# Half-tile squares ahead of entry splits in the inner norms, and modulation rows spread evenly over up and down

## The chip, the cores and the metric

One core of one Trainium2 chip runs the whole program. The metric is the device time of one execution in microseconds (us), the median of several runs. Engines: PE (TensorE) multiplies, ACT (ScalarE), DVE (VectorE) and POOL (GpSimd) work elementwise, SP issues the DMAs.

## The reference

A sequence of 512 tokens of width 1024 passes a first block (two layers of mixed attention) and a second block (two layers). The change touches only the second block. Cut to what matters:

```python
def second_block(x, c, w_ada, b_ada, norm_g, w_in, ..., w_out, w_up, conv_w, conv_b, w_down):
    for l in range(DEPTH):
        mod = jax.nn.silu(c) @ w_ada[l] + b_ada[l]
        sh1, sc1, g1, sh2, sc2, g2 = jnp.split(mod[:, None, :], 6, axis=-1)
        h = rms_norm_2(x, norm_g[l, 0]) * (1.0 + sc1) + sh1
        ...
        mix = jnp.concatenate([o_a, o_b, o_c], axis=-1) @ w_out[l]
        x = x + g1 * mix
        h = rms_norm_2(x, norm_g[l, 1]) * (1.0 + sc2) + sh2
        x = x + g2 * conv_ffn(h, w_up[l], conv_w[l], conv_b[l], w_down[l])
    return x
```

`rms_norm_2` divides each token by the root of its mean square over the 1024 channels. `conv_ffn` multiplies by `w_up` (1024 x 5632), convolves three neighbouring tokens, multiplies silu of one half by the other half (2816 channels, 22 tiles of 128), and multiplies by `w_down`.

## The kernel before, in words

**Tiling.** Channels lie on the 128 partitions, tokens along the free axis: x is XT, eight tiles of 128 channels by 512 tokens. Every product is made three times, with high and low parts: weights and values are split into a high part (rounded to fp32r) and the rest, and PE adds high x high, high x low and low x high (`channels`, line 695; `half_products`, line 887, for 256 tokens at a time).

**Weights.** PE's program builds a list `units`. Each unit is one DMA of 128x1024 numbers into one of three buffers RAW (unit n takes RAW[n % 3]; SP issues unit n once unit n-3 is done with it, in the order of the list, line 1760). For a weight, ACT copies the high part into WH, or into a spare tile X, Y or Z (line 1818), and POOL subtracts to get the low part (line 2447), which frees RAW; the ring of WH/WL has two places, given back when PE has used them. On ACT these splits stand at hand-placed points: `ahead(key, by)` issues all splits, in the order of the list, up to the weight of `key` and `by` further; a split that has been issued is not issued again.

**Modulation rows.** The sum silu(c) @ w_ada is made on DVE from rows of w_ada that pass through the same RAW ring as units of their own (not split): line 2742 for the first row of a chunk, line 2744 for the seven others. After eight rows a chunk of 1024 sums is transposed by PE (`modulation_columns`, line 738, eight transposes) and reduced on DVE (`modulation_biases`). In layer 0 of the second block 56 rows (`FEED_ROWS`) go beside up and down: `feed_rows` gives the rows behind up unit n = 2j + s (j over 22 tiles, s over the two halves of the product), `feed_rows_down` those behind unit i of down tile m (a down tile has three weights, i = 0, 1, 2).

**The norm that ends by halves** (`end_by_halves`, one function on each of PE, ACT and DVE). It is used three times: norm ("2",0,"n",1) after `wout` of layer 0, ("2",1,"n",0) after `down` of layer 0, and ("2",1,"n",1) after `wout` of layer 1. The last two output tiles, 6 and 7, are made in halves of 256 tokens:

- PE: (6, first half), (7, first half), then (6, second half) with the sums of squares of the first half in its middle (`half_sums`, lines 895 and 899), then the spread of the root (`half_spread`, line 908), (7, second half), and then three entry units together (line 948): up (0,0), (0,1), (1,0) in tiles X, or bff 0, bfb 0, bff 1 in tiles Y.
- DVE: updates x with each half (line 3101), adds the squares into ACC (line 3062), inverts the root, and writes the normalised value GV (line 3081) and the low part HL (line 3075) for each of eight tiles and both halves.
- ACT: squares the halves (line 2191), takes the root (line 2200), and writes the high part HH (line 1847). Before it, line 1873 loads the table that has the root (`load_root`).

Before the change ACT issues all splits up to the fourth entry unit, then the table load, and then the first square of a half tile.

Of the kernel before, what the change touches and what calls it, by code (L numbers as in the profile page):

```python
# [24 lines left out]
KD = DM // P  # L25
# [20 lines left out]
KF = DFF // P  # L46
# [123 lines left out]
FEED_ROWS = rows_of(("mod2", 0, MOD2_CHUNKS - 1), *[("mod2", 1, c) for c in range(MOD2_CHUNKS)])  # L170
# [25 lines left out]
def program(nc, D, out, known, stop=None):  # L196
    led = Ledger(known)
    up, at = led.up, led.at
    ctx = ExitStack()
    with ctx:  # L200
# [340 lines left out]
        def feed_rows(l, j, s):  # L541

            n = 2 * j + s
            if l or n < 5:
                return []
            return FEED_ROWS[2 * (n - 5):2 * (n - 5) + 2] if n < 10 else FEED_ROWS[n:n + 1]

        def feed_rows_down(l, m, i):

            n = 2 * KF + 2 * m + i  # L550
            return FEED_ROWS[n:n + 1] if l == 0 and i < 2 else []

        def completed(rows):

# [1252 lines left out]
        def _(act):  # L1807
# [18 lines left out]
            def freed(key):  # L1826
                return up(evacuated[led.slot(key)], key)
# [44 lines left out]
            def load_root():  # L1872
                A(SMALL[:, 7:8], epsb[:, 0:1], ACT.Sqrt)
# [304 lines left out]
                                 lambda s: MOD2[l][:, 24 * i + k:24 * i + k + 1],  # L2178
                                 (key, "rows") if k == KD - 1 else None)

            def end_by_halves(norm, name, following):

                _, l, _, i = norm

                def square_half(m, p):
                    if p:
                        value_is_there(None, name + (m,))
                    else:
                        act.wait_ge(dve_step, at(dve_step, (norm, "x", m)))
                    act.wait_ge(dve_step, at(dve_step, (norm, "add", m - 2)))  # L2190
                    A(SQ2[m % 2][:, half(p)], XT[:, m, half(p)], ACT.Square).then_inc(*up(act_out, (norm, "sq", m, p)))

                def shifted(p, k):
                    high_shifted(("2", l, "h", i, p, k), HH2[:, k, :], SEQ, lambda s: MOD2[l][:, 24 * i + k:24 * i + k + 1],
                                 (norm, "rows") if p and k == KD - 1 else None, [(0, HALF * p, HALF)])

                square_half(KD - 2, 0)
                square_half(KD - 1, 0)
                ps = ready((norm, 0))
                A(RCOL[:, 0:2], ps[:, 0:2], ACT.Sqrt, bias=epsb[:, 0:1], scale=1.0 / DM).then_inc(*freed((norm, 0)))  # L2200
                square_half(KD - 2, 1)
                for k in range(KD):
                    if k == 3:
                        square_half(KD - 1, 1)
                    if k == 5:
                        act.wait_ge(product_ready, at(product_ready, (norm, 1)))
                        A(RCOL[:, 2:4], psum[led.slot((norm, "rows"))][:, 1000:1002], ACT.Sqrt, bias=epsb[:, 0:1],
                          scale=1.0 / DM).then_inc(*up(act_out, (norm, 1, "root")))
                    shifted(0, k)
                for k in range(KD):  # L2210
                    shifted(1, k)
                ahead(following)
# [165 lines left out]
            def second_layer(l):  # L2378
                if l == 0:
                    for k in range(KD):  # L2380
                        if k == KD - 1:
                            keep_wide(("2", l, "n", 0), RSTD2, SEQ)
                        square2(l, 0, k, lambda k: updated_tile(act, 1, k), "tiles")
                    norm2(l, 0)
                recurrence(l)
                ahead(("2", l, "wout", 0))
                pair_attention(l, "a")
                pair_attention(l, "c")
                for j in range(3):
                    high(("2", l, "mix", "c", j), XH2[:, 5 + j, :], SEQ, ("2", l, "cyN", j))  # L2390
                for m in range(KD - 2):
                    ahead(("2", l, "wout", m))
                    square2(l, 1, m, lambda k: value_is_there(None, ("2", l, "out", k)), "DVE")
                ahead(("2", l, "wout", KD - 1), 4)
                load_root()
                end_by_halves(("2", l, "n", 1), ("2", l, "out"), ("2", l, "up", 1, 1))
                for j in range(KF):
                    for s in range(2):
                        key = ("2", l, "up", j, s)
                        ahead(key)  # L2400
                        U = (UA, UB)[s]
                        ps = ready(key)
                        if j:
                            act.wait_ge(split_value, at(split_value, ("2", l, "f", j - 1)))
                        c = s * KF + j
                        A(U[:, :], ps[:, 0:SEQ], ACT.Identity, bias=vec("conv_b", l, c),  # L2406
                          scale=vec("conv2", (l, 1), c)).then_inc(*up(act_out, ("2", l, "u", j, s)))
                    ahead(key, 2)
                    value_is_there(None, ("2", l, "up", j, 0))
                    A(UA[:, :], UA[:, :], ACT.Silu).then_inc(*up(act_out, ("2", l, "silu", j)))  # L2410
                    high(("2", l, "f", j), FH[:, j, :], SEQ)
                last = l == DEPTH - 1
                for m in range(KD if last else KD - 2):
                    for i in range(3):
                        ahead(("2", l, "down", m, i))
                    if not last:
                        square2(l + 1, 0, m, lambda k: value_is_there(None, ("2", l, "down", k)), "DVE")
                if not last:
                    ahead(("2", l, "down", KD - 1, 2), 4)
                    load_root()  # L2420
                    end_by_halves(("2", l + 1, "n", 0), ("2", l, "down"), ("2", l + 1) + FIRST_UNITS[3])

            if stop is None or stop[0] == "second":
                for l in range(DEPTH):
# [149 lines left out]
        def _(dve):  # L2574
# [519 lines left out]
            def end_by_halves(norm, name, gate):  # L3094

                l = name[1]

                def updated(m, p):
                    key, x = name + (m,), XT[:, m, half(p)]
                    dve.wait_ge(product_ready, at(product_ready, half_key(name, m, p)))  # L3100
                    ins = V.scalar_tensor_tensor(x, psum[led.slot(key)][:, 512 * p:512 * p + HALF],
                                                 MOD2[l][:, gate + m:gate + m + 1], x, ALU.mult, ALU.add)
                    if p:
                        ins.then_inc(*freed(key))
                        own(key)
                    else:
                        step(ins, (norm, "x", m))

                def second_update():
                    updated(KD - 1, 1)  # L3110
                    add_half(norm, KD - 2, 1)

                def second_root():
                    dve.wait_ge(act_out, at(act_out, (norm, 1, "root")))
                    V.reciprocal(RCOL[:, 2:4], RCOL[:, 2:4]).then_inc(*up(to_pe, (norm, 1, "rows")))

                updated(KD - 2, 0)
                add_half(norm, KD - 3)
                updated(KD - 1, 0)
                add_half(norm, KD - 2, 0)  # L3120
                own((norm, 0))
                V.reciprocal(RCOL[:, 0:2], RCOL[:, 0:2]).then_inc(*up(to_pe, (norm, 0, "rows")))
                updated(KD - 2, 1)
                apply_half(norm, 0, {2: second_update, 5: second_root})
                apply_half(norm, 1, {})
# [198 lines left out]
            def second_layer(l):  # L3324
# [25 lines left out]
                for j in range(KF):  # L3350
# [16 lines left out]
                    gv = value(("2", l, "f", j))  # L3367
                    V.tensor_tensor(gv[:, 0:SEQ], UA[:, :], UB[:, :], ALU.mult).then_inc(*valued(("2", l, "f", j)))  # L3368
                    dve.wait_ge(split_value, led.count[split_value.name])
                for i in range(2):  # L3370
                    modulation_rows(feed_rows_down(l, 0, i))
                last = l == DEPTH - 1
                norm = ("2", l + 1, "n", 0)
# [2 lines left out]
                for m in range(KD if last else KD - 2):  # L3376
                    key = ("2", l, "down", m)
                    dve.wait_ge(product_ready, at(product_ready, ("2", l, "down", m, 2)))
                    ps = psum[led.slot(key)]
                    x = XT[:, m, 0:SEQ]  # L3380
                    V.scalar_tensor_tensor(x, ps[:, 0:SEQ], MOD2[l][:, 40 + m:41 + m], x, ALU.mult, ALU.add).then_inc(  # L3381
                        *freed(key))
                    own(key)
                    if m >= 2 and not last:
                        add_half(norm, m - 1)
                    for i in range(2):
                        modulation_biases(feed_rows_down(l, m, i))
                        if m + 1 < KD:
                            modulation_rows(feed_rows_down(l, m + 1, i))
# [45 lines left out]
```

## Time and profile before

| | us |
|---|---|
| median of 3 runs | 3182.79 |
| lowest and highest | 3179.22, 3186.59 |
| the profiled execution | 3177.08 |
| its span | 3175.3 |
| PE busy in it | 3039.2 (96%) |
| DVE, ACT, POOL busy | 1536.3, 1186.6, 1063.1 |

The span is from the first to the last instruction; the execution's time is 1.8 us more. A matmul's record overlaps the next one's, so a busy PE says only that it had work. In the timeline a row has its start, its duration, engine and line, what it writes and reads, how many instructions are merged in it (x3), and in brackets the idle time of the engine before it with what ended that. PEclk, the granted TensorE clock, is 1.00 at full speed and 0.50 at half.

### The profile page before, as it was taken

How to read it: one execution, taken by the hardware profiler on the slowest of the kernel's cores; microseconds unless marked ns; L12 is line 12 of the kernel's file. 1: busy time of each engine (PE TensorE's matmuls, PEld its weight loads, DVE VectorE, ACT ScalarE, POOL GpSimd, SP SyncE). 2: the span in 40 equal slices, each digit the busy share in tenths (PEclk: the TensorE clock that was granted, in tenths of full speed). 3: DMA queues.
4: the chain of work that ended last, by engine and by line, in shares of the span. 5: the costliest groups of instructions: out<-in, count | busy, mean ns of one | idle time of the engine just before them, and what ended most of it. 6: DMA issues, size and time to landing. Idle time of an engine off the chain costs nothing.

```text
span 3175.3 us, 45245 instructions
## 1 busy us (share of the span) xinstructions
PE 3039.2 (96%) x18354; PEld 2472.1 (78%) x18354; DVE 1536.3 (48%) x1947; ACT 1186.6 (37%) x1937; POOL 1063.1 (33%) x509
## 2 busy tenths in 40 slices
PE   8999999999999999999999999899999999999999
PEld 6867688888888777788876776688888777788887
DVE  4364446462233586523314765377742875454520
ACT  3255421212224355432234445433432435444422
POOL 1302033323343301244452221335545221245553
PEclk9999999999999999999999999999999999999999
DMA  6201025342222233344332212246655112023332
GB/s 216 44 6 41 1 74 139 89 130 61 66 60 60 56 110 89 80 126 115 97 93 75 60 41 63 61 126 188 189 163 151 49 47 69 28 80 95 98 96 91
DMA packets 442379, 279.77 MB, mean 88 GB/s; under 512 B 113610, under 2 KB 419516, under 8 KB 441788
## 3 DMA queue, kind: packets, MB, share of 16 engines
q1 hardware_dynamic: 442172, 276.87, 31.1%
q8 instruction: 147, 2.41, 0.3%
q14 instruction: 60, 0.49, 0.0%
HBM read 274.73 MB, written 2.10 MB: 87 GB/s over the span
## 4 chain that ended last, share of the span: by engine, by line
PE 67%; DVE 4%; POOL 3%; ACT 3%; issue 2%; DMA 1%; DVEq 0%; ACTq 0%; POOLq 0%; SPq 0%
PE ps L695 45%; PE ps L1422 4%; POOL WL L2447 2%; PE ps L948 2%; PE ps L1498 2%; PE ps L1520 2%; PE ps L1491 1%; PE ps L1237 1%; PE ps L1563 1%; ACT WH L1818 1%; PE ps L1247 1%; PE ps L1264 1%; PE ps L1446 1%; PE ps L1594 1%; PE ps L1457 1%
## 5 line engine op out<-in xcount | busy, mean ns | idle before, releaser
L2447 POOL TENSOR_TENSOR WL<-RAW,WH 128x1024 fp32r<-128x1024 f32 (+2 forms) x344 | 827.3, 2405 | 1711.9 <-ACT WH L1818 1700.1
L695 PE MATMUL ps<-HH,WH 128*128 128x512 f32 x2136 | 709.5, 370 | 18.8 <-POOL WL L2447 17.3
L695 PE MATMUL ps<-HH,WL 128*128 128x512 f32 x2136 | 700.9, 366 | 0.0
L695 PE MATMUL ps<-HL,WH 128*128 128x512 f32 x2136 | 700.2, 365 | 0.0
L1818 ACT ACTIVATE WH<-RAW 128x1024 fp32r<-128x1024 f32 (+2 forms) x344 | 356.0, 1035 | 420.0 <-PE ps L695 269.4
L695 PEld LDWEIGHTS ps<-HH,WH 128*128 128x128 f32 x2136 | 367.4, 188 | 99.6 <-POOL WL L2447 25.8
L695 PEld LDWEIGHTS ps<-HH,WL 128*128 128x128 f32 x2136 | 366.4, 188 | 67.4
L695 PEld LDWEIGHTS ps<-HL,WH 128*128 128x128 f32 x2136 | 366.6, 188 | 65.7
L2744 DVE SCALAR_TENSOR_TENSOR XT<-RAW,CS,XT 128x1024 f32<-128x1024 f32 x77 | 129.2, 1677 | 22.5 <-DMA RAW<-in_w_ada 20.9
L695 PE MATMUL ps<-FH,WH 128*128 128x512 f32 x308 | 120.6, 392 | 2.0 <-POOL WL L2447 1.9
L695 PE MATMUL ps<-FH,WL 128*128 128x512 f32 x308 | 120.0, 390 | 0.0
L695 PE MATMUL ps<-FL,WH 128*128 128x512 f32 x308 | 120.0, 389 | 0.0
L2744 DVE SCALAR_TENSOR_TENSOR MSUM<-RAW,CS,MSUM 128x1024 f32<-128x1024 f32 x63 | 110.4, 1787 | 10.4 <-DMA RAW<-in_w_mod 8.7
L1422 PE MATMUL ps<-HH,WH 128*128 128x512 f32 x208 | 91.9, 442 | 3.8 <-POOL WL L2447 3.2
L3381 DVE SCALAR_TENSOR_TENSOR XT<-ps,MOD,XT 128x512 f32<-128x512 f32 x14 | 10.5, 750 | 167.9 <-PE ps L695 167.9
L1237 PE MATMUL ps<-KS,QS 128*128 128x512 f32 (+1 forms) x252 | 86.7, 480 | 3.5 <-ACT GV L1923 2.7
L2455 POOL TENSOR_TENSOR FL<-GV,FH 128x512 fp32r<-128x512 f32 x44 | 57.5, 1307 | 95.8 <-ACT FH L1840 95.8
L2835 DVE TENSOR_REDUCE NMAX<-ps 128x1 f32<-128x768 f32 (+1 forms) x80 | 65.9, 847 | 40.2 <-PE ps L1237 38.9
L1422 PE MATMUL ps<-HH,WL 128*128 128x512 f32 x208 | 82.9, 398 | 0.0
L1422 PE MATMUL ps<-HL,WH 128*128 128x512 f32 x208 | 82.8, 398 | 0.0
L2406 ACT ACTIVATE UB<-ps,VEC 128x512 f32<-128x512 f32 x44 | 34.3, 780 | 125.1 <-PE ps L695 125.1
L1840 ACT ACTIVATE FH<-GV 128x512 fp32r<-128x512 f32 x44 | 27.8, 632 | 141.0 <-DVE GV L3368 141.0
(493 smaller groups left out, 5550.4 us busy)
## 6 DMA issues: line engine op xcount, KB each, us to landing
RAW<-in_w_in SPq DMA_DIRECT2D x122, 512.0 KB, 3.9
RAW<-in_w_ada SPq DMA_DIRECT2D x96, 512.0 KB, 4.0
RAW<-in_w_up SPq DMA_DIRECT2D x88, 512.0 KB, 3.9
RAW<-in_w_in SPq DMA_DIRECT2D x72, 256.0 KB, 3.8
RAW<-in_w_mod SPq DMA_DIRECT2D x32, 512.0 KB, 3.7
RAW<-in_w_down SPq DMA_DIRECT2D x32, 512.0 KB, 3.7
WMOD<-in_w_mod SPq DMA_DIRECT2D x8, 1024.0 KB, 14.1
RAW<-in_w_branch SPq DMA_DIRECT2D x16, 512.0 KB, 3.4
```

The lines of the kernel that those rows point to most:

```text
L695: ins = nc.tensor.matmul(ps[0:width, t0:t0 + tn], a, b[:, k0 + k, tokens0 + t0:tokens0 + t0 + tn], start=first and k == 0 and i == 0, stop ...
L948: ins = nc.tensor.matmul(groups[n][:, half(p)], a, b[:, k, half(p)], start=k == 0 and t == 0, stop=k == KD - 1 and t == 2)
L1237: ins = nc.tensor.matmul(half[:, c:c + m], QS[:, 2 * j + h, qs], KS[2 * j + h][:, start:start + m], start=True, stop=True)
L1422: ins = nc.tensor.matmul(ps[:, 0:SEQ], lhs, rhs[:, k, 0:SEQ], start=k == 0 and i == 0, stop=k == KD - 1 and i == 2)
L1498: ins = nc.tensor.transpose(ps[:, b * P:(b + 1) * P], P2[n % 2][h][:, b * P:(b + 1) * P], ident)
L1520: ins = nc.tensor.matmul(o[hs, qb * P:(qb + 1) * P], VN2[a][:, b, hs], PT2[n % 2][h][:, b * P:(b + 1) * P], start=b == 0, stop=b == NXB - 1)
L1818: A(weight_tiles(units[n][3])[0][:, 0:used], RAW[n % NRAW][:, 0:used], ACT.Copy).then_inc(*up(w_high))
L2406: A(U[:, :], ps[:, 0:SEQ], ACT.Identity, bias=vec("conv_b", l, c), scale=vec("conv2", (l, 1), c)).then_inc(*up(act_out, ("2", l, "u", j, s)))
L2447: nc.gpsimd.tensor_tensor(wl[:, 0:used], RAW[n % NRAW][:, 0:used], wh[:, 0:used].bitcast(F32), ALU.subtract).then_inc(*up(w_low))
L2455: nc.gpsimd.tensor_tensor(L, GV[n % 2][:, 0:T], H.bitcast(F32), ALU.subtract).then_inc(*up(split_low, key))
L2744: V.scalar_tensor_tensor(total, row, c, total, ALU.mult, ALU.add).then_inc(*done)
L2835: V.tensor_reduce(NMAX[:, 2 * n + h:2 * n + h + 1], ps[:, 0:keys], AX.X, ALU.max, negate=True).then_inc(*up(to_act, ("B", l, n, h)))
```

## The change

Three edits, in ACT's order of work and in the placement of modulation rows. (1) After `wout`, the splits of tile 7's weight and of the first entry unit stand before the square of tile 5, instead of behind it. The table load stands directly behind that square; then come the split of the second entry unit, the square of tile 6, the split of the third, the square of tile 7, the root, and only then the split of the fourth, ahead of the second half's square. (2) After `down`, the table load stands before the three entry splits, both squares behind them, and the fourth split behind the root. (3) One modulation row goes behind every up unit from n = 5 on (before: two for n = 5 to 9, then one), so that unit n has row n - 5 instead of row n; the 17 rows left go behind all three units of a down tile (before: 12 rows, behind two of three). PE's, POOL's and SP's programs differ only by the place of the rows.

```diff
         def feed_rows(l, j, s):
 
             n = 2 * j + s
-            if l or n < 5:
-                return []
-            return FEED_ROWS[2 * (n - 5):2 * (n - 5) + 2] if n < 10 else FEED_ROWS[n:n + 1]
+            return FEED_ROWS[n - 5:n - 4] if l == 0 and n >= 5 else []
 
         def feed_rows_down(l, m, i):
 
-            n = 2 * KF + 2 * m + i
-            return FEED_ROWS[n:n + 1] if l == 0 and i < 2 else []
+            n = 2 * KF - 5 + 3 * m + i
+            return FEED_ROWS[n:n + 1] if l == 0 else []
...
-            def end_by_halves(norm, name, following):
+            def end_by_halves(norm, name, splits, following):
...
+                load_root()
+                ahead(splits[0], 0)
                 square_half(KD - 2, 0)
+                ahead(splits[1], 0)
                 square_half(KD - 1, 0)
                 ps = ready((norm, 0))
                 A(RCOL[:, 0:2], ps[:, 0:2], ACT.Sqrt, bias=epsb[:, 0:1], scale=1.0 / DM).then_inc(*freed((norm, 0)))
+                ahead(splits[2], 0)
                 square_half(KD - 2, 1)
...
                 for m in range(KD - 2):
-                    ahead(("2", l, "wout", m))
+                    ahead(("2", l, "wout", m), 1 if m < KD - 3 else 3)
                     square2(l, 1, m, lambda k: value_is_there(None, ("2", l, "out", k)), "DVE")
-                ahead(("2", l, "wout", KD - 1), 4)
-                load_root()
-                end_by_halves(("2", l, "n", 1), ("2", l, "out"), ("2", l, "up", 1, 1))
+                after = [("2", l, "up", j, s) for j in range(2) for s in range(2)]
+                end_by_halves(("2", l, "n", 1), ("2", l, "out"), after[1:4], after[3])
...
                 if not last:
-                    ahead(("2", l, "down", KD - 1, 2), 4)
-                    load_root()
-                    end_by_halves(("2", l + 1, "n", 0), ("2", l, "down"), ("2", l + 1) + FIRST_UNITS[3])
+                    ahead(("2", l, "down", KD - 1, 2), 0)
+                    after = [("2", l + 1) + unit for unit in FIRST_UNITS[0:4]]
+                    end_by_halves(("2", l + 1, "n", 0), ("2", l, "down"), (after[2], after[2], after[3]), after[3])
...
-                for i in range(2):
+                for i in range(3):
                     modulation_rows(feed_rows_down(l, 0, i))
...
-                    for i in range(2):
+                    for i in range(3):
                         modulation_biases(feed_rows_down(l, m, i))
                         if m + 1 < KD:
                             modulation_rows(feed_rows_down(l, m + 1, i))
```

## Rows read from the trace of the kernel before

**Rows 1.** The head of the page
```profile
span 3175.3 us, 45245 instructions
```

**Rows 2.** Timeline of PE, its gaps at the three norms (start, duration, ..., [idle before <- releaser])
```profile
2053.04 0.39 PE L887 MATMUL ps<-MIXH,WH 128*128 128x256 f32 x1 [2.10 <-POOL WL L2447]
2063.95 0.98 PE L895 MATMUL ps<-CONST,ACC 128*128 128x1 f32 x4 [6.33 <-DVE ACC L3062]
...
2456.67 0.98 PE L895 MATMUL ps<-CONST,ACC 128*128 128x1 f32 x4 [4.43 <-DVE ACC L3062]
...
2784.90 0.39 PE L887 MATMUL ps<-MIXH,WH 128*128 128x256 f32 x1 [2.09 <-POOL WL L2447]
2795.39 0.99 PE L895 MATMUL ps<-CONST,ACC 128*128 128x1 f32 x4 [4.44 <-DVE ACC L3062]
```

**Rows 3.** Timeline of ACT ahead of the first norm's root
```profile
2044.07 1.04 ACT L1818 ACTIVATE Z_H<-RAW 128x1024 fp32r<-128x1024 f32 x1
...
2049.50 1.05 ACT L1818 ACTIVATE WH<-RAW 128x1024 fp32r<-128x1024 f32 x1
...
2056.89 1.06 ACT L1818 ACTIVATE X_H<-RAW 128x1024 fp32r<-128x1024 f32 x1 [4.38 <-DMA RAW<-in_w_up]
2060.05 1.06 ACT L1818 ACTIVATE WH<-RAW 128x1024 fp32r<-128x1024 f32 x1 [2.10 <-DMA RAW<-in_w_up]
2061.12 1.28 ACT L1873 ACT_TABLE_LOAD   x1
...
2062.53 0.70 ACT L2191 ACTIVATE SQ<-XT 128x256 f32<-128x256 f32 x2
```

**Rows 4.** Timeline of POOL in the first norm, low half of tile 7's weight
```profile
2050.63 2.36 POOL L2447 TENSOR_TENSOR WL<-RAW,WH 128x1024 fp32r<-128x1024 f32 x1 [3.05 <-ACT WH L1818]
```

**Rows 5.** Timeline of DVE in the first norm
```profile
2051.57 1.97 DVE L3062 TENSOR_TENSOR ACC<-ACC,SQ 128x512 f32<-128x512 f32 x1
2056.29 0.48 DVE L3101 SCALAR_TENSOR_TENSOR XT<-ps,MOD,XT 128x256 f32<-128x256 f32 x1 [2.75 <-PE ps L887]
...
2068.59 0.48 DVE L3101 SCALAR_TENSOR_TENSOR XT<-ps,MOD,XT 128x256 f32<-128x256 f32 x1 [2.24 <-PE ps L887]
```

**Rows 6.** Timeline of SP's queue in the first norm: the DMA of up (1,0)
```profile
2053.01 0.37 SPq L1760 DMA_DIRECT2D RAW<-in_w_up  x1
```

**Rows 7.** Timeline of PE, third norm, second sums at full clock
```profile
2806.60 0.50 PE L895 MATMUL ps<-CONST,ACC 128*128 128x1 f32 x4
...
2807.41 0.36 PE L948 MATMUL ps<-HH,X_H 128*128 128x256 f32 x1
```

**Rows 8.** Windows, first norm: PE, PEld, DVE, ACT, POOL busy, PEclk, DMA share, GB/s
```profile
2064.00:2068.00 4.00, 4.00 (x19) 4.00 (x20) 0.17 (x1) 0.26 (x1) 0.00 (x0) 0.50 0.48 131
```

**Rows 9.** Timelines of ACT, POOL and DVE in the second norm
```profile
2445.14 3.11 ACT L1818 ACTIVATE Y_H<-RAW 128x1024 fp32r<-128x1024 f32 x3 [4.70 <-PE ps L1667]
...
2448.64 5.20 POOL L2447 TENSOR_TENSOR Y_L<-RAW,Y_H 128x1024 fp32r<-128x1024 f32 x2
...
2450.91 0.48 DVE L3101 SCALAR_TENSOR_TENSOR XT<-ps,MOD,XT 128x256 f32<-128x256 f32 x1 [1.66 <-PE ps L887]
```

**Rows 10.** Timelines of ACT and PE in up: units 5, 11, 43, one chunk's transposes
```profile
2107.53 0.78 ACT L2406 ACTIVATE UB<-ps,VEC 128x512 f32<-128x512 f32 x1 [1.61 <-PE ps L695]
...
2149.66 0.78 ACT L2406 ACTIVATE UB<-ps,VEC 128x512 f32<-128x512 f32 x1 [2.79 <-PE ps L695]
...
2328.97 0.78 ACT L2406 ACTIVATE UB<-ps,VEC 128x512 f32<-128x512 f32 x1 [2.53 <-PE ps L695]
...
2130.79 1.04 PE L738 MATMUL ps<-CONST,XT 128*128 128x128 f32 x8
```

**Rows 11.** Timelines of PE, DVE and ACT in down
```profile
2341.30 0.50 PE L695 MATMUL ps<-FH,WH 128*128 128x512 f32 x1 [1.13 <-POOL WL L2447]
...
2380.88 3.19 DVE L2744 SCALAR_TENSOR_TENSOR XT<-RAW,CS,XT 128x1024 f32<-128x1024 f32 x1 [0.71 <-DMA RAW<-in_w_ada]
...
2388.89 1.06 ACT L1818 ACTIVATE WH<-RAW 128x1024 fp32r<-128x1024 f32 x1 [4.62 <-PE ps L695]
```

## The prediction

> **What bounds the kernel now.** I read the page first, then the PE timeline for its idle gaps, then ACT, POOL, DVE and SP around each. PE decides the time, so only gaps in PE, and stretches in which it is granted its lower clock, can be won. In the second block five gaps belong to the three norms that end by halves [rows 2]: before the first norm (layer 0, after `wout`) PE waits 2.10 us for the low half of the last weight tile and 6.33 us for the square sums; the third norm (layer 1, after `wout`) repeats it with 2.09 and 4.44; the second (after `down`) has 4.43 alone. The reader is to see who ends these waits: DVE's addition into ACC, which waited for ACT's squares. In the first norm ACT squares at 2062.53 what DVE had updated at 2056.29 + 0.48 = 2056.77 [rows 3, 5]. In between ACT did splits of entry weights (2056.89 and 2060.05, both after waiting for a DMA) and a table load. That is the stall. After it PE runs at half clock: 0.50, the lower of its two levels (1.2 GHz), over 2064 to 2068 [rows 8].
>
> The up stage of layer 0 has a loss of its own. Unit n's output is taken by ACT at 2107.53 (n=5), 2149.66 (n=11) and 2328.97 (n=43) [rows 10]. From 11 to 43 there are 32 units and four finished chunks, each of these with eight transposes of 1.04 us in all [rows 10]: (179.31 - 4.16) / 32 = 5.47 us a unit, and one modulation row a unit is carried without loss. From 5 to 11, with two rows a unit, six units and one chunk take 42.13 where 6 x 5.47 + 1.04 = 33.9 would do: 8.2 us lost.
>
> **Part 1, first norm.** The splits of tile 7 and of up (0,0) now come before the square of tile 5. Between tile 6's split (2044.07 + 1.04) and that square, straight before 2049.50, ACT had nothing to do [rows 3]. Its buffer was given back with tile 4, so I put it at 2045.1 to 2046.1 and up (0,0) behind it to 2047.2; the square still comes on time, about 2049. POOL then works without a pause, at 2.36 us a tile [rows 4]: tile 6's low half from 2045.2 to 2047.6, tile 7's to 2049.95, up (0,0) from there. So tile 7's low half is there 1 us before PE wants it at 2050.94: the 2.10 us go. ACT's table load and root take 1.28 + 0.2 from 2049.5 to 2051.0 [rows 3], in time that was idle or is now free.
> The DMAs move as well, since SP reuses a RAW buffer when POOL is done with it: up (1,0) was issued at 2053.01, as tile 7's split ended, and ACT took it at 2056.89, 3.9 us later [rows 6, 3]. Now it is issued at 2049.95 and is there at 2053.8. Its split (1.06) holds ACT to 2054.9, and the square of tile 7's first half follows to 2055.3.
> PE: 24 + 12 products take from 2053.04 to the stall at 2063.95 - 6.33 = 2057.62, 0.127 us each [rows 2]. Starting at 2050.95 it reaches the sums at 2055.5. DVE updates the tile at 2054.2 to 2054.7 and then must add with both inputs in SBUF. What that costs beside POOL: the 128x512 addition at 2051.57 ended at 2053.54, only after POOL's operation of 2050.63 to 2052.99 [rows 4, 5]. The third split POOL then has at hand (up (0,1), ready at 2052.6) ends at about 2055.5, and the addition at 2055.8. PE begins the sums at 2055.95: 0.4 us of stall are left. Shift 2.10 + 6.33 - 0.4 = 8.0.
> On this pair of engines the Trainium skill ("SBUF — State Buffer", section "Who interferes with whom") says that the later of the two fully blocks until the other's instruction is done. The trace agrees; it speaks against the change, since more POOL splits now lie next to DVE's adds. By it alone the addition could stand behind two splits instead of one, which is the second rival.
> Clock: from the sums to DVE's update of the next half are 2068.59 - 2063.95 = 4.64 us [rows 2, 5]. At full clock the sums take 2807.41 - 2806.60 = 0.81 [rows 7], twelve products 1.53 and the hand-over 0.1: 2.4. A 0.4 us stall should not lower the clock, so 2.2 more. The fourth split (up (1,1)) now stands behind the root, ahead of the second half's square. Its DMA (issued when up (0,0)'s split ends, 2052.6, there by 2056.5) is earlier than the end of the root, 2055.95 + 0.81 + 0.3 = 2057.1; the split lasts to 2058.2, and DVE's update, on which the next square waits, to 2055.95 + 2.4 + 0.48 = 2058.8. So ACT loses nothing, with 0.6 in hand. But POOL's 2.36 us now run while DVE writes the first HL half, again with two SBUF inputs: I count 0.3 between 0 and one whole split, 2.4. Sum: 8.0 + 2.2 - 0.3 = 9.9.
> **Part 1, third norm.** The same with its own rows: 2.09 + 4.44, and the way between its two stalls took 2795.39 - 4.44 - 2784.90 = 6.05 where the first norm took 4.58, so 1.5 was lost to the clock. 8.0 - 0.4 + 2.2 - 0.3 = 9.5.
> **Part 1, second norm.** Only the fourth split leaves the way, and the table load goes ahead of the three Y splits. These are done at 2448.25, DVE's update of tile 7 at 2450.91 + 0.48 = 2451.39 [rows 9]. POOL does the last two Y splits from 2448.64 to 2453.84, so it changes over at about 2451.5. If the addition (issued at 2451.43) gets in between, the sums meet PE at 2452.24 and the whole 4.43 and the clock's 2.2 are won, less 0.3: 6.3. If not, it ends at 2454.15: 2.4 won, and of the 2.2 about a half, since a gap of 2.1 us was once followed by the low clock (third norm) and once not (first): 3.2. The trace can't tell; I take 4.7.
> **Part 2, rows.** One row a unit from n=5 on: the 8.2 us go, as after n=11. Up finishes one chunk fewer (1.04 less), down one more. Row 39's chunk now ends behind unit (0,0) of down, where PE waits for DVE's row. The unit ends at 2328.97 + 5.47 = 2334.4; DVE comes to the row only behind the last product of up. I put the wait at 0.7, between 0 and 2. With the transposes that is 1.7, but PE then stalls less at 2341.30, where it waits 1.13 for a split [rows 11]. The reduction of that chunk on DVE, 1024 columns as a row has, stands ahead of the row whose buffer tile 1's third weight needs: up to 0.9. Together 8.2 + 1.0 - 1.7 + 1.1 - 0.9 = 7.7.
> Every down tile now carries three rows in three units. A row can hold DVE for 3.19 us behind POOL [rows 11]; the next tile's first weight waits for the second row's buffer: from the row's end at 2384.07 plus 3.9 it is there at 2388.0, and ACT takes the next tile's first weight at 2388.89, when PE gives back the slot [rows 11]. So it is just covered, by 0.9; with that cover gone each tenth of a microsecond counts, in five tiles. I count nothing, the range 0 to 4.
>
> **Sum.** 9.9 + 9.5 + 4.7 + 7.7 = 31.8. The profiled execution took 3177.1 (span 3175.3 [rows 1]); it would take 3145.3. The median of the runs lies 5.7 above it, so I set 3182.8 - 31.8 = 3151.
>
> **Rivals.** (1) The forecast: chance 0.60, 3143 to 3159 by the terms' ends (second norm 3.2 or 6.3, down 0 to 4, stalls 0 to 1, runs differing by 4).
> (2) The addition comes behind POOL's next split: 2.36 us more in norms one and three, and with gaps of some 2.7 the clock falls again (2.2 each), with the second norm at 3.2: 9.1 + 1.5 = 10.6 less, 3162. For it: adds and splits are within 0.8 us. Against: in the trace the waiting addition gets in at the first change-over. 0.18.
> (3) The third row per down tile brings back what the second row a unit cost in up: 1.4 us for each of six units there, once or twice in each of five tiles, 7 to 14 less: 3158 to 3165. Against it: two DMAs a unit, not three. 0.12.
> (4) It doesn't do what it says: the square of tile 7 stays behind a weight whose DMA lands 3 us or more after my 2053.8, because transfers that now follow 2.4 us apart share the engines. Then the gaps stay, and only part 2 is won: 3175. Against: landing took 3.9 at a like density. 0.06.
> (5) Slower: the ring of three RAW buffers locks to DVE's rows in down. If the next weight is issued only after the row that follows the tile's own update, its DMA, split and POOL pass (3.9 + 1.06 + 2.36 = 7.3) lie open in each of five tiles, 36.6 in all: 3151 + 37 = 3188. It decides when the third row is eaten later than the end of the next tile, 15 us; I find 11. 0.04.
>
> Range: leaving out (4) and (5) and the far end of (3), 3142 to 3166. A difference of 0.2%, 6.4 us, is about what a measurement can tell: faster 0.93, same 0.04, slower 0.03.
>
> **What would show it.** Right: no PE gap over 1 us ahead of tile 7 in norms one and three; sums there 0.4 us late; clock 1.00 throughout; ACT's squares 0.1 us after DVE's updates or after the split of up (1,0); no PE gap in up between n=5 and n=11; gaps in down below 1.2 us each, as the one in [rows 11]. Wrong: a gap of 2 us and more at the sums behind a POOL pass (2), PE waiting for `down` weights whose DMA follows a row (3, 5), ACT waiting for RAW between the two squares (4).

## The result and the profile after

The changed kernel takes 3152.26 us (median of five runs, 3150.69 to 3155.84); in the same session the kernel before took 3179.22 to 3187.32, and the ratio is 0.9901 (95% interval 0.9889 to 0.9912). One run of the kernel before, of 6019 us, and one of the rows alone below, of 7639 us, were disturbed and are outside the ratios. The forecast was 3151, the range 3142 to 3166.

The profiled execution took 3152.26; its page begins so, where the kernel before had 3175.3 [rows 1]:

```profile
span 3150.5 us, 45245 instructions
PE 3037.7 (96%) x18354; PEld 2466.8 (78%) x18354; DVE 1544.4 (49%) x1947; ACT 1186.1 (38%) x1937; POOL 1065.5 (34%) x509
```

Work and counts are the same; what shrank is waiting, and the time that PE spent at its lower clock. **Where the time went** is read best by taking the same PE instruction in both traces and subtracting its start: the number changes only in a stretch that became shorter or longer. Steps of that difference, in us, worked out from the PE timelines of each kernel against the one of the kernel before:

| stretch | after | squares alone | rows alone | 4th split early | 4th split late | both squares first |
|---|---|---|---|---|---|---|
| first block and all up to the first norm | +6.8 | -3.7 | +7.9 | +0.9 | +2.9 | +4.5 |
| first norm, to the sums | -7.9 | -8.0 | -0.2 | -7.9 | -8.0 | -8.9 |
| first norm, behind the sums | -2.6 | -2.6 | +0.1 | +0.9 | -2.5 | -2.4 |
| entry and up, to n = 5 | -1.0 | +0.2 | -1.1 | -1.1 | -0.5 | +1.1 |
| up, n = 5 to 11 | -7.9 | +2.4 | -7.7 | -7.9 | -7.8 | -7.9 |
| up, n = 11 to the start of down | +1.0 | +0.8 | +1.4 | +0.8 | +0.9 | +0.9 |
| down | +0.1 | 0.0 | +1.5 | +1.9 | -0.4 | -0.5 |
| second norm, to the sums | -4.6 | -4.6 | -0.1 | -4.6 | -4.6 | -4.6 |
| second norm, behind them | -2.5 | -2.5 | +1.1 | +0.5 | -2.6 | -2.5 |
| between second and third norm | +3.3 | -0.5 | +3.2 | +2.1 | +1.6 | +0.5 |
| third norm, to the sums | -7.5 | -7.5 | 0.0 | -7.5 | -7.5 | -8.4 |
| third norm, behind them | -2.0 | -2.0 | +0.7 | +1.0 | -2.1 | +0.5 |
| from there to the end | 0.0 | 0.0 | 0.0 | 0.0 | +0.6 | +1.2 |

In the changed kernel the stretches that the change touches give 10.5 (first norm), 7.8 (up and down), 7.1 and 9.5: 34.9 together. The two rows of untouched work give back 10.1 in this one execution. The first differs from -3.7 to +7.9 over kernels whose code is the same there, so it is the spread of executions and no effect; the medians have less of it. ("Rows alone" is read from its second run, the one with a usable trace.)

PE's gaps at the three norms, as [rows 2] (timeline of PE, the kernel after; ACC is the sum of squares):

```profile
2062.78 0.58 PE L893 MATMUL ps<-CONST,ACC 128*128 128x1 f32 x4 [0.75 <-DVE ACC L3063]
...
2440.57 0.50 PE L893 MATMUL ps<-CONST,ACC 128*128 128x1 f32 x4
...
2772.61 0.58 PE L893 MATMUL ps<-CONST,ACC 128*128 128x1 f32 x4 [0.76 <-DVE ACC L3063]
```

The gaps of 2.10 and 2.09 for tile 7's weight are gone without a row of their own, 6.33 has become 0.75, 4.43 nothing, 4.44 has become 0.76. ACT in the first norm, as [rows 3], and POOL, as [rows 4]:

```profile
2050.84 1.04 ACT L1816 ACTIVATE Z_H<-RAW 128x1024 fp32r<-128x1024 f32 x1
2051.78 1.04 ACT L1816 ACTIVATE WH<-RAW 128x1024 fp32r<-128x1024 f32 x1
2052.73 1.04 ACT L1816 ACTIVATE X_H<-RAW 128x1024 fp32r<-128x1024 f32 x1
2055.74 0.63 ACT L1857 ACTIVATE SQ<-XT 128x512 f32<-128x512 f32 x1 [1.96 <-DVE XT L3345]
2056.39 1.28 ACT L1871 ACT_TABLE_LOAD   x1
...
2058.17 1.06 ACT L1816 ACTIVATE X_H<-RAW 128x1024 fp32r<-128x1024 f32 x1 [0.29 <-DMA RAW<-in_w_up]
2059.13 0.40 ACT L2189 ACTIVATE SQ<-XT 128x256 f32<-128x256 f32 x1
2061.09 1.06 ACT L1816 ACTIVATE X_H<-RAW 128x1024 fp32r<-128x1024 f32 x1 [1.55 <-DMA RAW<-in_w_up]
2062.05 0.40 ACT L2189 ACTIVATE SQ<-XT 128x256 f32<-128x256 f32 x1
...
2056.68 8.19 POOL L2448 TENSOR_TENSOR X_L<-RAW,X_H 128x1024 fp32r<-128x1024 f32 x3
```

Three splits stand back to back ahead of tile 5's square, the table load sits in idle time, and the two half-tile squares follow one split each. Tile 7's square comes at 2062.05, 0.87 after DVE's update of 2060.70 + 0.48; in the kernel before the two squares began 5.8 after it. The window behind the sums, as [rows 8], is at the full clock:

```profile
2064.00:2068.00 4.00, 4.00 (x36) 4.00 (x35) 2.54 (x6) 2.50 (x5) 3.27 (x2) 1.00 0.82 240
```

DVE in the first and the second norm, as [rows 5] and [rows 9], with POOL in the second:

```profile
2060.70 0.48 DVE L3102 SCALAR_TENSOR_TENSOR XT<-ps,MOD,XT 128x256 f32<-128x256 f32 x1 [0.60 <-PE ps L885]
2061.22 1.42 DVE L3063 TENSOR_TENSOR ACC<-ACC,SQ 128x256 f32<-128x256 f32 x1
...
2067.03 0.78 DVE L3076 SCALAR_TENSOR_TENSOR HL<-GV,MOD,HH 128x256 fp32r<-128x256 f32 x1
...
2439.92 0.43 DVE L3063 TENSOR_TENSOR ACC<-ACC,SQ 128x256 f32<-128x256 f32 x1
...
2434.77 7.82 POOL L2448 TENSOR_TENSOR Y_L<-RAW,Y_H 128x1024 fp32r<-128x1024 f32 x3 [2.96 <-ACT Y_H L1816]
```

The same addition takes 1.42 behind a POOL pass and 0.43 where it meets a change-over (three passes from 2434.77 in 7.82: the second change-over is at about 2440.0). In up PE has no gap above 0.05 between n = 5 and n = 11, and unit 5 and unit 11 lie 32.98 apart where [rows 10] had 42.13 (ACT takes their outputs). Of these 9.15 the table has 1.1 in the row above n = 5, since its cut there stands behind the first of the gaps that went:

```profile
2103.88 0.78 ACT L2407 ACTIVATE UB<-ps,VEC 128x512 f32<-128x512 f32 x1 [3.06 <-PE ps L693]
...
2136.86 0.78 ACT L2407 ACTIVATE UB<-ps,VEC 128x512 f32<-128x512 f32 x1 [2.53 <-PE ps L693]
```

In down, as [rows 11], PE waits 0.36 for the row whose chunk it transposes. The product that waited 1.13 in the kernel before starts at 2329.91 without any idle time, so that wait is gone. The next wait for a split, 0.43 in the kernel before, is 0.48:

```profile
2323.51 1.09 PE L736 MATMUL ps<-CONST,XT 128*128 128x128 f32 x8 [0.36 <-DVE XT L2745]
...
2329.91 0.39 PE L693 MATMUL ps<-FH,WH 128*128 128x512 f32 x1
...
2340.09 0.50 PE L693 MATMUL ps<-FH,WH 128*128 128x512 f32 x1 [0.48 <-POOL WL L2448]
```

The last of these in the kernel before:

```profile
2351.55 0.50 PE L695 MATMUL ps<-FH,WH 128*128 128x512 f32 x1 [0.43 <-POOL WL L2447]
```

### The profile page after: what moved, and what is told of

It reads as the page before. It is cut to its first block, busy times and chain, and to the rows that moved or that the text cites. A ratio compares the mean times of both kernels' runs of the same rounds, so it can differ in the third digit from the quotient of the medians.

```text
span 3150.5 us, 45245 instructions
## 1 busy us (share of the span) xinstructions
PE 3037.7 (96%) x18354; PEld 2466.8 (78%) x18354; DVE 1544.4 (49%) x1947; ACT 1186.1 (38%) x1937; POOL 1065.5 (34%) x509
## 3 DMA queue, kind: packets, MB, share of 16 engines
q1 hardware_dynamic: 442172, 276.87, 31.5%
## 4 chain that ended last, share of the span: by engine, by line
PE 68%; DVE 3%; POOL 3%; ACT 3%; issue 2%; DMA 1%; SPq 0%; DVEq 0%; ACTq 0%; POOLq 0%
PE ps L693 46%; PE ps L1420 4%; POOL WL L2448 2%; PE ps L946 2%; PE ps L1496 2%; PE ps L1518 2%; PE ps L1489 1%; PE ps L1235 1%; PE ps L885 1%; PE ps L1561 1%; ACT WH L1816 1%; PE ps L1245 1%; PE ps L1262 1%; PE ps L1303 1%; PE ps L1592 1%
## 5 line engine op out<-in xcount | busy, mean ns | idle before, releaser
L2745 DVE SCALAR_TENSOR_TENSOR XT<-RAW,CS,XT 128x1024 f32<-128x1024 f32 x77 | 140.7, 1827 | 31.2 <-DMA RAW<-in_w_ada 30.2
L3382 DVE SCALAR_TENSOR_TENSOR XT<-ps,MOD,XT 128x512 f32<-128x512 f32 x14 | 10.5, 751 | 141.5 <-PE ps L693 141.5
```

The source lines that it names most:

```text
L2745: V.scalar_tensor_tensor(total, row, c, total, ALU.mult, ALU.add).then_inc(*done)
```

## The experiments

My theory: the gain is ACT's squares no longer waiting behind splits (some 27 us in three norms, 2 us of each being the clock that no longer falls), and 7 to 8 us of modulation rows. Against it stood: one part gives all; the clock part isn't the stall's; the fourth split's place doesn't matter; and a third row in down costs. Ratios are to the kernel before, run beside each.

**Each part alone.** The squares' order with the rows as before, and the rows with the old order (cut; DVE's loops over a down tile's rows go with it, two or three times):

```diff
 squares alone (against after)          rows alone (against before)
-return FEED_ROWS[n - 5:n - 4] ...     +return FEED_ROWS[n - 5:n - 4] if l == 0 and n >= 5 else []
+return FEED_ROWS[2 * (n - 5):...]     -return FEED_ROWS[2 * (n - 5):...]
-n = 2 * KF - 5 + 3 * m + i            +n = 2 * KF - 5 + 3 * m + i
+n = 2 * KF + 2 * m + i                -n = 2 * KF + 2 * m + i
```

> The new order of squares and splits alone; modulation rows placed as in the kernel before. Theory (three separate gains that add): the three norms gain what the changed kernel's trace shows, 10.4, 7.1 and 9.5 us, so 27 us less than before in all; up between units 5 and 11 keeps its loss of 8.2 us, PE gaps of 1 to 2 us with rows' DMAs among them, and down its gap of 1.1 us in tile 0. Rival (the two edits hang together, since rows that come earlier take RAW buffers while the norm's last splits need them): the first norm gains less than 9 us.

> The new placement of modulation rows alone; ACT's order in the norms as before. Theory: up between units 5 and 11 gains 9.0 us (8.2 of gaps and half clock, 0.8 for a chunk that moves), up to unit 43 and down give back about 1, 7.9 us less than before in all. The three norms keep gaps at the sums of 6.3, 4.4 and 4.4 us and half clock after them. Rival: a third row in every down tile makes a gap per tile, and less than 4 us are left.

> The new placement of modulation rows alone, once more for a trace of it. Theory: between the last tile of wout in layer 0 and unit 11 of up the step against the kernel before is -9 us, all of it between units 5 and 11; from unit 11 to the end of down it is +1 at most; the steps at the three norms are zero. Rival (the third row of a down tile costs): a PE gap over 1 us in each of down's tiles 1 to 5.

The squares alone: 3158.91, ratio 0.9915 (0.9895 to 0.9934), that is 27.1 us of 3184. The rows alone: 3179.68, ratio 0.9979 (0.9967 to 0.9990), 6.7 us. They ran once more for a trace (3183.99 in that one execution). The two add to 33.8, and the whole change measured 31.5 (0.0099 x 3184), with intervals of 3 to 6 us on each: the parts add up within what is measured. The table says the same by stretches: the norms' steps stand in the first alone, up's in the second. From the last tile of `wout` to n = 11 the rows alone step by -8.9, near the -9 that was expected; from there to the end of down by +2.9, where +1 at most was expected, and the bullet on the rows below says of what. Behind the sums of the second and the third norm, where nothing was expected, it has +1.1 and +0.7. No tile of down from 1 to 5 has a gap over 1. Rows alone keeps its gaps at the sums (PE, first norm):

```profile
2071.65 0.98 PE L894 MATMUL ps<-CONST,ACC 128*128 128x1 f32 x4 [6.19 <-DVE ACC L3061]
```

The squares alone keep double rows in up, and lose 2.4 more there than the kernel before, in longer gaps. That PE now comes sooner to a ring that is no faster would explain it, but isn't shown by itself (PE, up of layer 0, squares alone):

```profile
2094.43 0.50 PE L695 MATMUL ps<-HH,WH 128*128 128x512 f32 x1 [1.11 <-POOL WL L2450]
2101.83 0.50 PE L695 MATMUL ps<-HH,WH 128*128 128x512 f32 x1 [1.66 <-POOL WL L2450]
2109.78 0.50 PE L695 MATMUL ps<-HH,WH 128*128 128x512 f32 x1 [2.21 <-POOL WL L2450]
2117.11 0.50 PE L695 MATMUL ps<-HH,WH 128*128 128x512 f32 x1 [0.70 <-POOL WL L2450]
2125.25 0.50 PE L695 MATMUL ps<-HH,WH 128*128 128x512 f32 x1 [2.41 <-POOL WL L2450]
```

**The fourth split ahead of tile 7's first square**, the last place the old order had it in:

```diff
                 ahead(splits[1], 0)
+                ahead(splits[2], 0)
                 square_half(KD - 1, 0)
...
-                ahead(splits[2], 0)
                 square_half(KD - 2, 1)
```

> The changed kernel with one step undone: ACT issues the fourth split ahead of the square of tile 7's first half, instead of behind the root. Theory (what holds the sums back is the square behind a split whose DMA has not landed): in the second norm the gap before the sums comes back as some 2.2 us (square at about 2454.3 on the scale of the kernel before, PE ready at 2452.2), in the first and third it grows from 0.75 to 2.5 to 3, each with up to 2.2 more by half clock: 6.6 to 13 us slower than the changed kernel. Rival (POOL's hold on DVE's addition is what was won, ACT's order is not): the addition still gets in where it did, and the kernel is at most 2 us slower.

3161.57, ratio 0.9935 (0.9915 to 0.9956): 9.3 us slower than after (10.8 by the ratios). The other moves of ACT's order, the early splits of tile 7 and the earlier table load, were not undone one by one. PE starts the sums as in after, with the same 0.75, but now waits inside them for the square, which stands behind a split that waits for its DMA: 1.79 in the first norm, 1.35 in the third, and 1.39 in the second, where 2.2 was expected (PE in the first and the second norm, then ACT in the first):

```profile
2056.88 0.58 PE L893 MATMUL ps<-CONST,ACC 128*128 128x1 f32 x4 [0.75 <-DVE ACC L3063]
2059.24 0.61 PE L897 MATMUL ps<-CONST,SQ 128*128 128x1 f32 x4 [1.79 <-ACT SQ L2189]
...
2441.58 0.61 PE L897 MATMUL ps<-CONST,SQ 128*128 128x1 f32 x4 [1.39 <-ACT SQ L2189]
...
2057.83 1.06 ACT L1816 ACTIVATE WH<-RAW 128x1024 fp32r<-128x1024 f32 x1 [1.45 <-DMA RAW<-in_w_up]
2058.79 0.40 ACT L2189 ACTIVATE SQ<-XT 128x256 f32<-128x256 f32 x1
```

Two gaps of 0.75 and 1.79 with 0.6 of tiny products between them were followed by a lower clock (0.57 in the next window, the kernel with the early fourth split):

```profile
2060.00:2064.00 4.00, 4.00 (x23) 4.00 (x22) 1.48 (x4) 0.91 (x3) 1.33 (x1) 0.57 0.84 232
```

The three norms lose 3.5, 3.0 and 3.0 from the start of the sums on, 9.5 in all, near what the medians have. Of each, 1.79, 1.39 and 1.35 is the wait itself and the other 1.6 to 1.7 the lower clock.

**The clock alone.** The kernel before, with 18 useless products of 512 columns on PE ahead of the wait for the sums; nothing comes sooner:

```diff
             def half_sums(norm, p, ps, c, warm=None):
+                if warm is not None:
+                    keep_going(ps, warm, 18)
```

> The kernel before with 18 added 512-column products of no use on PE at each norm, put into an unused PSUM half just before the wait for the square sums, 4.1 us of work inside gaps of 6.3, 4.4 and 4.4 us. They change no wait. Theory (2.2 to 2.5 us of each norm's gain is the half clock that follows the gap): from the sums to DVE's next update there are 2.4 us instead of 4.64 in the second and third norm and perhaps the first, whose gap still has 2.2 us: 4.5 to 7 us less than before, with all sums starting when they did. Rival (the slow stretch is not due to the gap): 4.64 us stay, and the time does not move.

3179.89, ratio 0.9990 (0.9980 to 0.9999): 3.2 us, where 4.5 to 7 were expected. In the second norm the products cover the stall to 0.21, the sums don't move (-0.1), and the stretch behind them is 2.4 shorter: just the clock's part, as in after (2.5). In the first and the third norm they left 2.15 and 2.05 of the stall, and the clock's part came only to 1.0 and 0.5. The third norm's stall was also 1.5 longer to begin with, as in the rows alone (5.90 there): behind the 2.1 for tile 7's weight the clock stayed up in these two, PE came sooner to the sums, and they began no sooner. PE, warm kernel:

```profile
2065.59 0.61 PE L897 MATMUL ps<-CONST,ACC 128*128 128x1 f32 x4 [2.15 <-DVE ACC L3064]
...
2458.63 0.61 PE L897 MATMUL ps<-CONST,ACC 128*128 128x1 f32 x4 [0.21 <-DVE ACC L3064]
```

So about 2.4 us of a norm belong to the clock, shown by itself in the second norm alone. In these traces it came in full with gaps of 0.75 and less. The length of a gap doesn't decide it: the lower clock followed one of 1.39 above, and the last experiment below has a gap of 2.01 that it did not follow.

**Two rows a unit put back, later.** After, with two rows behind each of the units 20 to 29 and two instead of three in a down tile:

```diff
+            first = n - 5 + min(max(n - 20, 0), 10)
+            return FEED_ROWS[first:first + (2 if 20 <= n < 30 else 1)]
```

> The changed kernel, with two modulation rows a unit at ten units of up, 20 to 29, and one at the others from 5 on; down has seven rows instead of 17. Theory (the loss is of two rows a unit, wherever they stand: three DMAs and three users share a ring of three RAW buffers): no loss from 5 to 19, PE gaps of 1 to 2.5 us from 20 to 31, and 1.4 to 1.8 us lost a double unit, 14 to 18 in all, some 15 us slower than the changed kernel; down runs no faster without its ten rows. Rival (the loss belonged to the start of up, where the pipeline has just been filled behind the norm): no gaps at 20 to 29, within 2 us of the changed kernel.

3169.05, ratio 0.9946 (0.9929 to 0.9962), 17 us slower than after (14 by the ratios). PE's gaps above 0.1 stand at these units and those straight behind them, and nowhere else in up (first ones):

```profile
2190.78 0.50 PE L696 MATMUL ps<-HH,WH 128*128 128x512 f32 x1 [1.09 <-POOL WL L2451]
2198.72 0.50 PE L696 MATMUL ps<-HH,WH 128*128 128x512 f32 x1 [2.16 <-POOL WL L2451]
```

From n = 11 to n = 36 this kernel's step is 21.4 larger than that of after; one more chunk's transposes are 1.0 of it, so ten double units cost 2.0 each, more than the 1.4 to 1.8 that I had expected (8.2 for five units in the kernel before is 1.6). Part of this is the clock: it fell behind three of the gaps here and behind one of those in the kernel before, at 1.6 each by the products that then start 0.43 apart instead of 0.23 (window of the first, this kernel):

```profile
2200.00:2203.00 3.00, 3.00 (x8) 2.31 (x7) 2.78 (x4) 0.44 (x1) 0.00 (x0) 0.50 0.99 287
```

Without it a double unit costs 1.6 here and 1.3 there. Ahead of the gap of 2.16, while the next weight's DMA is under way (issued at 2190.75), DVE waits 3.19 for the DMA of two rows and does them; only then does it write the value GV for which ACT waits, and the split of the weight stands behind ACT's work on that (DVE, then ACT):

```profile
2189.76 3.42 DVE L2748 SCALAR_TENSOR_TENSOR XT<-RAW,CS,XT 128x1024 f32<-128x1024 f32 x2 [3.19 <-DMA RAW<-in_w_ada]
...
2193.99 0.63 ACT L1841 ACTIVATE FH<-GV 128x512 fp32r<-128x512 f32 x1 [5.19 <-DVE GV L3372]
2195.20 1.05 ACT L1819 ACTIVATE WH<-RAW 128x1024 fp32r<-128x1024 f32 x1
```

So the loss is of two rows a unit, wherever they stand. How much of it is the ring's (a row takes a buffer ahead of the next weight) and how much the order of work on DVE isn't separated. In down its step is some 1.6 less than that of after, and down has two chunks' transposes fewer there. Behind the first tile of down after has one gap that this kernel lacks, 0.37, so the third row of a down tile costs no more than that.

**The fourth split later still**, between the two loops of the shifted value:

```diff
-                ahead(splits[2], 0)
                 square_half(KD - 2, 1)
...
                     shifted(0, k)
+                ahead(splits[2], 0)
```

> The changed kernel with the fourth split a little later, behind all high halves of the first half of the tokens, so that POOL's pass no longer lies beside DVE's first low half. Theory (DVE has slack there, PE has other products to do): HL's first write takes 0.48 instead of 0.78 us, PE's steps at the norms stay within 0.2 us, the time is the same. Rival (that contention costs what was booked, 0.3 a norm, or delays the entry): 1 us less in all, or, where the pass now hits the second half's low halves, PE gaps at the entry.

3152.1, ratio 0.9892 (0.9877 to 0.9906): the same as after. The first HL write, 0.78 in after, is 0.48, but the steps at and behind the sums don't change: the 0.3 was slack. Instead POOL's pass meets a later HL write, which PE does wait for (DVE, POOL, PE, late fourth split):

```profile
2063.16 0.48 DVE L3076 SCALAR_TENSOR_TENSOR HL<-GV,MOD,HH 128x256 fp32r<-128x256 f32 x1
...
2073.00 2.16 DVE L3076 SCALAR_TENSOR_TENSOR HL<-GV,MOD,HH 128x256 fp32r<-128x256 f32 x1
...
2072.47 2.41 POOL L2448 TENSOR_TENSOR WL<-RAW,WH 128x1024 fp32r<-128x1024 f32 x1 [11.40 <-ACT WH L1816]
...
2075.22 0.39 PE L946 MATMUL ps<-HH,X_H 128*128 128x256 f32 x1 [0.30 <-DVE HL L3076]
```

**Both squares ahead of the second and third split**, to win the last 0.75 (norms after `wout`; `i == 0` is the norm after `down`, which stays as it was):

```diff
                 load_root()
-                ahead(splits[0], 0)
+                if i == 0:
+                    ahead(splits[1], 0)
                 square_half(KD - 2, 0)
-                ahead(splits[1], 0)
                 square_half(KD - 1, 0)
+                ahead(splits[1], 0)
```

> The changed kernel with the second and third entry splits behind both half-tile squares in the norms after wout (the norm after down as it is). Theory (what is left of the gap before the sums, 0.75 us in the first and third norm, is DVE's addition waiting for POOL's pass on the second entry weight, and nothing of ACT): with POOL idle by then the addition takes 0.42 instead of 1.42 us and the gap is gone, 1.5 us in two norms; but POOL's two passes then lie beside DVE's low halves and the same lock gives back 0.5 to 2 us a norm at the entry. Between 1.5 us faster and 2.5 slower than the changed kernel. Rival (the 0.75 us come from ACT's square of tile 7, late behind the third split): same gap, since only the addition counts, or the gap shrinks with the addition's time unchanged.

3151.3, ratio 0.9894 (0.9880 to 0.9909): the same again. The addition takes 0.42, the gap at the sums is gone, 0.9 won in each of the two norms. It is lost again at the entry: POOL's passes now lie beside the HL writes, DVE's update of the last half is late, and PE waits 2.01 for it, in the first norm as in the third (DVE, POOL, PE, first norm, both squares first):

```profile
2058.95 0.42 DVE L3064 TENSOR_TENSOR ACC<-ACC,SQ 128x256 f32<-128x256 f32 x1
...
2063.88 1.55 DVE L3077 SCALAR_TENSOR_TENSOR HL<-GV,MOD,HH 128x256 fp32r<-128x256 f32 x1 [0.25 <-ACT HH L1845]
...
2065.99 1.95 DVE L3077 SCALAR_TENSOR_TENSOR HL<-GV,MOD,HH 128x256 fp32r<-128x256 f32 x1
2067.86 0.47 DVE L3103 SCALAR_TENSOR_TENSOR XT<-ps,MOD,XT 128x256 f32<-128x256 f32 x1
...
2060.39 4.76 POOL L2449 TENSOR_TENSOR X_L<-RAW,X_H 128x1024 fp32r<-128x1024 f32 x2 [3.12 <-ACT X_H L1816]
...
2068.48 0.35 PE L946 MATMUL ps<-HH,X_H 128*128 128x256 f32 x1 [2.01 <-DVE XT L3103]
```

Two HL writes end 0.3 behind a POOL pass (which end at 2065.15 and 2067.65) and take 1.07 and 1.47 more than the 0.48 of a free one. Whoever moves POOL's passes away from the additions moves them onto these writes. By the table the first norm wins 0.9 up to the sums against after and loses 2.1 at its entry; the third wins 0.9 and loses 2.5 behind the sums and 1.2 later, since there the lower clock followed the gap of 2.01; in the first norm it did not. Such a loss of some 4 us in one execution isn't seen in the medians, whose intervals are as wide.

## Why the prediction held, point by point

- **The stall of the squares** was sized and placed rightly. Forecast 9.9 and 9.5 for the first and the third norm, measured 10.5 and 9.5. Tile 7's weight wait went as computed: POOL was done with its low half and began the next pass at 2056.68, which is 2049.9 in the time of the kernel before (this execution lay 6.77 behind), where 2049.95 was forecast. The gap at the sums is 0.75 and not 0.4, but the sums begin at 2062.78 - 6.77 = 2056.01, as forecast (2055.95): PE only came to them 0.24 sooner. The DMA of up (1,0) was there 0.5 later than I had it (2061.09 - 6.77 = 2054.3 against 2053.8), which cost nothing: tile 7's square ended at 2062.45, before the addition at 2062.64, and PE's row names the addition. The first norm's 0.6 more is the clock (2.6, not 2.2) and the 0.3 for POOL beside the first HL write, which wasn't paid. The clock's term ended at DVE's update of 2068.59, but in the kernel before the clock stood at 0.50 until 2069.4 at least.
- **The second norm** was the mis-sized term: 4.7 forecast, 7.1 measured. I had taken the middle between the addition getting in at POOL's change-over (6.3) and not (3.2), since the trace couldn't tell. It got in, and closely: the row at 2439.92 has 0.43, some 0.1 or less from POOL's change-over; PE has no gap, and in all six kernels with this order the step to the sums is -4.6. The part above 6.3 is the clock (2.5, not 2.2) and the 0.3 for POOL beside the first HL write, which cost nothing in any norm. The late fourth split showed this: the write took 0.48 instead of 0.78 and no step moved.
- **The clock's part**, 2.2 a norm: 2.6, 2.5 and 2.0, seen by itself in the second norm of the warm kernel (2.4). The early fourth split gave back 1.6 to 1.7 of it in each.
- **The rows**: 7.7 forecast, 7.8 by the trace, and this nearness is luck: two misses cancel. Up gave 8.9 to n = 11, near the 8.2 and one chunk (1.04) that were computed. Then +1.0 came that I hadn't counted. It is the rows': up finishes four chunks behind n = 11 in both kernels, but they moved from units 15, 23, 31 and 39 to 12, 20, 28 and 36. Where they stand now each puts the next product off by 0.8; where they stood PE now has a wait of 0.2 that they had covered, so each move costs 0.2, 0.8 in all. What that wait is for stays open. The rows alone show the same at the same places, and +0.5 for one gap besides; the +0.8 of the squares alone is a single gap of 0.59 and has nothing to do with it. Down was forecast 1.5 worse and was 0.1: the wait for the row (0.36, where I had 0.7) and the transposes put PE off by 1.4 together, the gap of 1.13 went to nothing and gave 1.4 back, and the 0.9 for the reduction ahead of tile 1's third weight didn't come (PE's wait in that tile went from 0.43 to 0.48). That the gap of 1.13 goes is not the same in each execution: with the same rows it was 1.25 in the rows alone and 1.49 in the early fourth split, which is most of their +1.5 and +1.9 in down, so the term of down lies between 0 and 2. Why it goes in some and not in others stays open.
- **Rival 2** (addition behind the next split) fell: the addition ended at the first change-over it met, after 1.42 in the first and third norm and after 0.43 in the second. **Rival 3** (third row in down) fell, twice over: squares alone against after, and the double-row kernel. **Rival 4** (square behind a late DMA) fell: the split was 0.5 late and not 3, and the 0.75 are the addition's wait for POOL; with the addition free of it, both squares first, that gap is gone. **Rival 5** (ring locked to DVE's rows in down) fell: no PE gap in down of the kernel after is over 0.8, and the longest in any other kernel is 1.49, where it has 7.3.
- **The sum**: 31.8 forecast; 31.5 by the ratio, 34.9 by the touched stretches of one execution. Measured against its own execution the forecast of 3145.3 missed by 7.0: 10.1 came from stretches that the change doesn't touch, and the touched ones gave 3.1 more. The median was met since such spread averages out in medians, and by some luck: the second norm gave 2.4 more than forecast, and the interval of the ratio alone is 7 us wide. How much of a single trace's difference is spread is only seen by cutting it at the edges of the change.

## What to carry to other kernels

An operation that a chain of dependent engines waits for should stand on its engine ahead of work that itself waits for a DMA, even where that work is short: the wait is the price, not the work. When the work that ends a stall is moved, price the clock with it: here a third of what the second norm gained and a fifth to a quarter of the others' came from PE no longer falling to 1.2 GHz. Gaps of 0.75 and less gave it in full; with longer ones, from 1.39 to 2.2, the lower clock followed in some cases and not in others. And a per-unit load that fits once but not twice (one row a unit here) should be spread evenly over all units that have room before any gets a second.

## What the runs showed of the hardware

- DVE's two-input operations in SBUF wait for POOL's pass in hand and get in at its end, even when POOL has passes queued back to back: 1.42 and 0.43 for the same addition, 1.55, 1.95 and 2.16 for an HL write that takes 0.48 alone. The Trainium skill ("SBUF — State Buffer", section "Who interferes with whom") calls it an exclusive lock between the two; the rows agree, and show besides that the lock changes hands at each pass. POOL pays too: three passes took 8.19 in the first norm where three of 2.36 [rows 4] would be 7.1.
- The same gap of PE isn't always followed by the same clock. Between the second and the third norm PE waits 2.13 for a split, in code that no kernel here changes. Behind it the clock stayed at its higher level in the squares alone, and fell for a part of the window in after (windows of the two, straight behind that gap, which ends at 2478.93 and at 2478.24):

```profile
2479.00:2483.00 4.00, 4.00 (x18) 3.31 (x19) 3.86 (x5) 0.31 (x1) 2.43 (x1) 1.00 0.45 134
```

```profile
2479.00:2483.00 4.00, 4.00 (x12) 3.09 (x12) 3.86 (x5) 0.00 (x0) 2.09 (x1) 0.59 0.57 165
```

In five of the nine traces it fell behind this gap. That alone is 1.6 of the +3.3 in the table. Most of the rest is a stretch at the lower clock that lasted 10 us in after (from 2639.3) and 7 in the kernel before (from 2656.6). The longer waits of other places show no order by length either: the lower clock followed the single 1.39 in the second norm of the early fourth split, and one of the two gaps of 2.01 with both squares first. The gaps of 0.75 and 1.79, and of 0.75 and 1.35, close together in the first and the third norm of the early fourth split, were followed by it too; one of 0.75 by itself never was.
